# Stick-breaking attention whose mask and tail are summed in PSUM, with two sets of banks, three heads in flight, and a convolution that begins one stage earlier

## The reference, cut to what matters

```python
def stick_breaking_attention(q, k, v):          # 512 tokens, 8 heads of 64
    z = jnp.einsum("bqhd,bkhd->bhqk", qb, kb) * scale
    mask = s_idx < t_idx
    log_beta = jax.nn.log_sigmoid(z)
    log_one_minus = jnp.where(mask, jax.nn.log_sigmoid(-z), 0.0)
    tail = lax.cumsum(log_one_minus, axis=3, reverse=True) - log_one_minus
    weights = jnp.where(mask, jnp.exp(log_beta + tail), 0.0)
    outs.append(jnp.einsum("bhqk,bkhd->bqhd", weights, vb))
...
attn = stick_breaking_attention(q, k, v).reshape(bsz, seq, ATTN_WIDTH)
c = glu_a * jax.nn.sigmoid(glu_b)
c = causal_depthwise_conv(c, conv_dw_w[layer], conv_dw_b[layer])     # 31 taps, 512 channels
c = jax.nn.silu(layer_norm(c, conv_ln_g[layer], conv_ln_b[layer]))
mixed = jnp.concatenate([attn, c], axis=-1) @ w_out[layer]
```

## Time and profile before

| | |
|---|---|
| three runs | 3109.27, 3105.01, 3108.11 us; median 3108.11 |
| the profiled execution | 3104.05 us, span 3102.3 us, granted clock 0.96 |
| busy share of the span | PE 93%, PEld 76%, DVE 48%, ACT 32%, POOL 45% |
| 156 us to 327 us from the start: busy | PE 103.93, DVE 139.95, ACT 72.72, POOL 89.74 of 171.00 us, granted clock 0.78 |

### The profile page before, as it was taken

How to read it: one execution, slowest core, us unless ns; L and a number is a source line. 1 busy time by engine, 2 the same in 40 slices (tenths; PEclk the granted TensorE clock), 3 DMA queues, 4 the chain that set the end, 5 groups by cost and what they waited for, 6 DMA issues and landing times.

```text
span 3102.3 us, 35547 instructions
## 1 busy us (share of the span) xinstructions
PE 2888.4 (93%) x13578; PEld 2348.8 (76%) x13578; DVE 1501.8 (48%) x2421; ACT 995.7 (32%) x1447; POOL 1393.4 (45%) x550
## 2 busy tenths in 40 slices
PE   7956799998998989988998999999999999999997
PEld 5733587886795668776887888888888888888886
DVE  3189432122117541546978788650002555555554
ACT  3234332223115542333333333332223223222322
POOL 5492254454320014443346777774445444444441
PEclk9968899999996999989999999999999999999999
DMA  3200122322420002321243654655455666556662
GB/s 124 92 3 0 41 82 88 102 89 74 151 82 14 1 28 95 108 82 55 75 143 103 207 158 156 207 176 185 147 196 170 195 191 195 193 189 190 195 195 70
DMA packets 222319, 375.90 MB, mean 121 GB/s; under 512 B 11152, under 2 KB 142608, under 8 KB 211216
## 3 DMA queue, kind: packets, MB, share of 16 engines
q1 hardware_dynamic: 222224, 374.68, 36.8%
HBM read 305.43 MB, written 69.21 MB: 121 GB/s over the span
## 4 chain that ended last, share of the span: by engine, by line
PE 77%; DVE 8%; issue 7%; POOL 5%; ACT 2%; DMA 0%; POOLq 0%; SPq 0%; DVEq 0%; ACTq 0%
PE bank L254 15%; PE bank L255 15%; PE bank L256 15%; PE bank L1831 8%; PE bank L1832 8%; PE bank L1833 8%; POOL rows_b L1647 4%; DVE cacc L433 2%; PE bank L1163 2%; PE bank L1134 2%; PE bank L1811 1%; PE bank L1143 1%; POOL u_lo L1611 1%; DVE xl L397 1%; PE bank L1753 0%
## 5 line engine op out<-in xcount | busy, mean ns | idle before, releaser
L246 POOL TENSOR_TENSOR w_lo<-w_raw,w_hi 128x2048 fp32r<-128x2048 f32 (+2 forms) x96 | 418.4, 4360 | 804.3 <-ACT w_hi L241 804.2
L1998 DVE TENSOR_TENSOR h_lo<-h_raw,h_hi 128x512 fp32r<-128x512 f32 x128 | 308.9, 2413 | 351.3 <-ACT h_hi L1633 351.3
L1628 POOL TENSOR_TENSOR v_lo<-v_raw,v_hi 128x1024 fp32r<-128x1024 f32 x128 | 308.0, 2407 | 377.4 <-ACT v_hi L1624 377.4
L1611 POOL TENSOR_TENSOR u_lo<-u_raw,u_hi 128x1024 fp32r<-128x1024 f32 x128 | 325.0, 2539 | 338.9 <-ACT u_hi L1605 338.9
L254 PE MATMUL bank<-xh,w_lo 128*128 128x512 f32 x1056 | 421.6, 399 | 38.5 <-DVE xl L397 18.1
L255 PE MATMUL bank<-xl,w_hi 128*128 128x512 f32 x1056 | 417.3, 395 | 0.0
L256 PE MATMUL bank<-xh,w_hi 128*128 128x512 f32 x1056 | 416.6, 395 | 0.0
L254 PE MATMUL bank<-xh,u_lo 128*128 128x512 f32 x1024 | 404.4, 395 | 0.3 <-POOL u_lo L1611 0.3
L1831 PE MATMUL bank<-h_hi,v_lo 128*128 128x512 f32 x1024 | 399.6, 390 | 4.2 <-DVE h_lo L1998 4.2
L1832 PE MATMUL bank<-h_lo,v_hi 128*128 128x512 f32 x1024 | 399.3, 390 | 0.0
L1833 PE MATMUL bank<-h_hi,v_hi 128*128 128x512 f32 x1024 | 399.3, 390 | 0.0
(11 more groups left out here) (338 smaller groups left out, 4492.4 us busy)
## 6 DMA issues: line engine op xcount, KB each, us to landing
w_raw<-w_small SPq DMA_DIRECT2D x80, 1024.0 KB, 4.9
u_raw<-expert_u SPq DMA_DIRECT2D x128, 512.0 KB, 3.7
v_raw<-expert_v SPq DMA_DIRECT2D x128, 512.0 KB, 5.1
h_scratch<-h_act SPq DMA_DIRECT2D x128, 256.0 KB, 2.2
g_scratch<-stage SPq DMA_DIRECT2D x8, 4096.0 KB, 16.7
h_raw<-h_scratch SPq DMA_DIRECT2D x128, 256.0 KB, 2.7
g_in<-g_scratch SPq DMA_DIRECT2D x64, 512.0 KB, 4.1
w_raw<-w_small SPq DMA_DIRECT2D x8, 768.0 KB, 4.3
```

The costliest lines, as they stand in the source:

```text
L246: pool.tensor_tensor(wl[g % 2][:, :n], raw[g % 2][:, :n], wh[g % 2][:, :n].bitcast(F32), ALU.subtract).then_inc(sem("lo_done"), 1)
L1611: pool.tensor_tensor(u_lo[c % 2][:, :, :], u_raw[c % 4][:, :, :], u_hi[c % 2][:, :, :].bitcast(F32), ALU.subtract)\
L1628: pool.tensor_tensor(v_lo[c % 4][:, :], v_raw[c % 4][:, :], v_hi[c % 4][:, :].bitcast(F32), ALU.subtract)\
L1998: dve.tensor_tensor(h_lo[c % 4][:, :], h_raw[c % 4][:, :], h_hi[c % 4][:, :].bitcast(F32), ALU.subtract)\
```

## The change

It does five things.

1. Scores, mask and tail of a head are summed in the same PSUM banks. After the four score matmuls, four bf16 matmuls of an identity with a constant add -2^100 where a key is not before its query. `tails` adds minus the softplus over the key itself and all later ones (`from_key`, `all_keys`) to the same banks. ACT takes the Exp straight from PSUM. With that `lbeta`, `log_weights` and both masks on DVE go.
2. Even heads use banks 4 to 6, odd heads banks 0 to 2; `scores(h+2)` waits until the weights of head h have been read.
3. The order of the heads: PE runs `tails(h)`, `values(h-1)`, `scores(h+2)`; ACT the weights of h, the output of h-1, `pre(h+2)`; DVE 12 instructions of the convolution and `softplus(h+2)`.
4. DVE begins the convolution in the `in_v` stage, three instructions after each of the eight copies, 24 in all. POOL begins its group before it prepares the two first blocks of `out1`, not after. The inverses are spread in the order of the pairs of heads, and only after all eight tiles of `in_v` have been copied.
5. The rounding of the attention's output for `out1` goes with each second head, and three of the four low parts are taken before the layer norm's reciprocal. PE takes the mean after the values of head 5. Three constants more are written at the start.

```diff
+        def head_banks(h):
+            return (lin_bank if h % 2 else att_bank)[:3]
+
+        PAIR_ORDER = (0, 4, 1, 5, 2, 6, 3, 7)
...
                 if h >= 1:
-                    act.wait_ge(sem("st_zread"), h)
+                    act.wait_ge(sem("st_soft"), h)
                 for b, (off, w) in enumerate(PIECES):
-                    ins = act.activation(ln1[:, off:off + w], att_bank[b][:, :w], ACT.Abs)
...
+            def weights_out(h):
+
+                act.wait_ge(sem("st_tail"), h + 1)
+                if h >= 2:
+                    act.wait_ge(sem("st_pv"), h - 1)
+                for b, (off, w) in enumerate(PIECES):
+                    ins = act.activation(wgt[h % 2][:, off:off + w], head_banks(h)[b][:, :w], ACT.Exp)
+                ins.then_inc(sem("st_w"), 1)
...
+                if h % 2:
+                    act.wait_ge(sem("st_o"), h + 1)
+                    act.activation(xh[:, k, :], attn[:, k, :], ACT.Copy).then_inc(sem("mix1_hi"), 1)
...
             pre(0)
-            for h in range(HEADS + 1):
-                if h + 1 < HEADS:
-                    pre(h + 1)
...
+            pre(1)
+            for h in range(HEADS):
+                weights_out(h)
                 if h >= 1:
-                    r = (h - 1) % 2 * HD
-                    act.wait_ge(sem("st_pv"), h)
-                    act.activation(attn[r:r + HD, (h - 1) // 2, :], lin_bank[3][r:r + HD, :], ACT.Copy)\
-                       .then_inc(sem("st_o"), 1)
+                    head_out(h - 1)
+                if h + 2 < HEADS:
+                    pre(h + 2)
...
+            head_out(HEADS - 1)
...
-            act.wait_ge(sem("st_o"), HEADS)
-            for k in range(CT):
-                act.activation(xh[:, k, :], attn[:, k, :], ACT.Copy).then_inc(sem("mix1_hi"), 1)
...
-            for b in range(1, LAYER["out1"]["block"] + 2):
...
             wait(pool, ("bank_free", 4 + 16), ("params_loaded", 16))
             conv_pool(pool)
-            for b in range(LAYER["out1"]["block"] + 2, LAYER["up0"]["block"] + 2):
+            for b in range(LAYER["out1"]["block"], LAYER["up0"]["block"] + 2):
...
-            for j in range(8):
-                if j >= 2:
-                    pe.wait_ge(sem("qk_ready"), j - 1)
-                pe.matmul(att_bank[1 + j % 2][:, :], head_spread[:, j * P:(j + 1) * P], rstd16[:, :],
...
+            pe.wait_ge(sem("bank_free"), 4 + LAYER["in_v"]["tile"] + 8)
+
+            def spread(first, last):
+                for n in range(first, last):
+                    j = PAIR_ORDER[n]
+                    if n >= 2:
+                        pe.wait_ge(sem("qk_ready"), n - 1)
+                    pe.matmul((att_bank, lin_bank)[n % 2][3][:, :], head_spread[:, j * P:(j + 1) * P], rstd16[:, :],
+                              start=True, stop=True).then_inc(sem("qk_spread"), 1)
...
-                pe.wait_ge(sem("qk_ready"), 8)
-                if h >= 1:
-                    pe.wait_ge(sem("st_zread"), h)
+                pe.wait_ge(sem("qk_ready"), 2 * t + 2)
...
                 for kb in range(QT):
                     b, c, w = regions(kb)
-                    last = pe.matmul(att_bank[b][:, c:c + w], qk[r:r + HD, 4 + t, kb * P:(kb + 1) * P],
-                                     qk[r:r + HD, t, kb * P:S], start=True, stop=True)
+                    bank = head_banks(h)[b]
+                    pe.matmul(bank[:, c:c + w], qk[r:r + HD, 4 + t, kb * P:(kb + 1) * P], qk[r:r + HD, t, kb * P:S],
+                              start=(c == 0), stop=False, skip_group_check=True)
+                for kb in range(QT):
+                    b, c, w = regions(kb)
+                    last = pe.matmul(head_banks(h)[b][:, c:c + P], ident_b[:, :], not_before[:, :], start=False, stop=True,
+                                     skip_group_check=True)
                 last.then_inc(sem("st_z"), 1)
...
                 pe.wait_ge(sem("st_soft"), h + 1)
-                if h >= 1:
-                    pe.wait_ge(sem("st_logw"), h)
-                else:
-                    pe.wait_ge(sem("bank_free"), 4 + LAYER["in_v"]["tile"] + 8)
                 for kb in range(QT):
                     b, c, w = regions(kb)
...
                         wj = S - jb * P
-                        last = pe.matmul(lin_bank[b][:, c + w - wj:c + w], later_key[:, :] if jb == kb else ones[:, :],
-                                         soft[h % 2][:, KOFF[jb]:KOFF[jb] + wj], start=(jb == kb), stop=(jb == QT - 1))
+                        last = pe.matmul(head_banks(h)[b][:, c + w - wj:c + w], from_key[:, :] if jb == kb else all_keys[:, :],
+                                         soft[h % 2][:, KOFF[jb]:KOFF[jb] + wj], start=False, stop=True, skip_group_check=True)
                 last.then_inc(sem("st_tail"), 1)
...
                 r = h % 2 * HD
-                pe.wait_ge(sem("st_wm"), h + 1)
+                pe.wait_ge(sem("st_w"), h + 1)
...
+            spread(0, 4)
             scores(0)
-            for h in range(HEADS + 1):
-                if h + 1 < HEADS:
-                    scores(h + 1)
-                if h < HEADS:
-                    tails(h)
-                if h == HEADS:
-                    variance()
+            spread(4, 8)
+            pe.wait_ge(sem("qk_ready"), 8)
+            scores(1)
+            for h in range(HEADS):
+                tails(h)
                 if h >= 1:
                     values(h - 1)
-                if h == HEADS - 1:
+                if h + 2 < HEADS:
+                    scores(h + 2)
+                if h == HEADS - 2:
                     mean()
+            values(HEADS - 1)
+            variance()
...
+            dve.wait_ge(sem("bank_free"), 4 + 16)
...
-            for j in range(8):
-                dve.wait_ge(sem("qk_spread"), j + 1)
+                conv_dve(dve, 3 * n, 3 * n + 3)
+            for n, j in enumerate(PAIR_ORDER):
+                dve.wait_ge(sem("qk_spread"), n + 1)
                 gain = qg[:, 0:1] if j < 4 else col("k_norm")
-                dve.scalar_tensor_tensor(out=qk[:, j, :], in0=qk[:, j, :], scalar=gain, in1=att_bank[1 + j % 2][:, :],
+                dve.scalar_tensor_tensor(out=qk[:, j, :], in0=qk[:, j, :], scalar=gain, in1=(att_bank, lin_bank)[n % 2][3][:, :],
                                          op0=ALU.mult, op1=ALU.mult).then_inc(sem("qk_ready"), 1)
...
                 for b, (off, w) in enumerate(PIECES):
-                    ins = dve.scalar_tensor_tensor(out=soft[h % 2][:, off:off + w], in0=att_bank[b][:, :w], scalar=0.0,
+                    ins = dve.scalar_tensor_tensor(out=soft[h % 2][:, off:off + w], in0=head_banks(h)[b][:, :w], scalar=0.0,
                                                    in1=ln1[:, off:off + w], op0=ALU.max, op1=ALU.add)
-                for b, (off, w) in enumerate(PIECES):
-                    ins = dve.scalar_tensor_tensor(out=lbeta[h % 2][:, off:off + w], in0=att_bank[b][:, :w], scalar=0.0,
-                                                   in1=ln1[:, off:off + w], op0=ALU.min, op1=ALU.subtract)
-                ins.then_inc(sem("st_zread"), 1)
-                dve.wait_ge(sem("st_zread"), h + 1)
-                mask_diagonals(soft[h % 2]).then_inc(sem("st_soft"), 1)
...
-                for b, (off, w) in enumerate(PIECES):
-                    ins = dve.tensor_tensor(wgt[h % 2][:, off:off + w], lbeta[h % 2][:, off:off + w],
-                                            lin_bank[b][:, :w], ALU.subtract)
-                ins.then_inc(sem("st_logw"), 1)
+                ins.then_inc(sem("st_soft"), 1)
 
             softplus(0)
-            per_head = -(-N_CONV // (HEADS - 1))
-            for h in range(HEADS + 1):
-                conv_dve(dve, h * per_head, (h + 1) * per_head)
-                if h >= 1:
-                    dve.wait_ge(sem("st_w"), h)
...
+            softplus(1)
+            per_head = -(-(N_CONV - 24) // (HEADS - 2))
+            for h in range(HEADS - 2):
+                conv_dve(dve, 24 + h * per_head, 24 + (h + 1) * per_head)
+                softplus(h + 2)
...
+            for k in range(CT - 1):
+                mixed_low(k)
             dve.wait_ge(sem("ln_std"), 1)
             chain.link(dve.reciprocal(ln_rstd[:, :], ln_std[:, :]))
             for k in range(CT):
                 dve.tensor_tensor(cacc[:, k, :], cacc[:, k, :], ln_rstd[:, :], ALU.mult).then_inc(sem("ln_y"), 1)
-                mixed_low(k)
+                if k == 0:
+                    mixed_low(CT - 1)
...
+            step(pool.memset(all_keys[:, :], -1.0))
+            step(pool.affine_select(out=from_key[:, :], in_=all_keys[:, :], compare_op=ALU.is_ge, fill=0.0, base=0,
                                     pattern=[[-1, P]], channel_multiplier=1))
-            step(pool.affine_select(out=causal[:, :], in_=ones[:, :], compare_op=ALU.is_gt, fill=0.0, base=0,
+            step(pool.memset(not_before[:, :], 0.0))
```

(2 more changed lines are left out.)

48 lines of the change are left out of this document (18 added, 30 removed).

## The result

| | before | changed |
|---|---|---|
| median of the runs on one chip | 3106.56 us | 3059.61 us (3058.56 to 3063.07, four runs) |
| ratio | | 0.9854, 95% interval 0.9841 to 0.9866 |
| the profiled execution, span | 3104.05, 3102.3 us | 3063.07, 3061.3 us |
| layer norm's reciprocal starts | 326.53 us | 279.86 us |
| first residual addition of `out1` | 339.72 us | 292.05 us |

The account below looks back on a forecast made before the run. The prediction took DVE's full queue to bound the attention stage. 49.2 us gained up to the reciprocal, plus 1.0 in out1, less 0.9 for constants, made 49.3 us from 3108.11: forecast 3058 us, range 3046 to 3078.

Parts of the forecast that it names:

- The cause: Attention heads' stage: DVE's full queue bounds it, so the 40.7 us of work removed there shorten the time.
- The start: From in_v to softplus(1): scores of head 0 about 5 us later, DVE idle twice, 20 us in sum, softplus(1) done at 187.2.
- the constants: Three more constants written on POOL at the kernel's start, on the path: 0.6 to 1.5 us, taken as 0.9.
- The heads: Softplus(2) to softplus(7): DVE needs 14.75 us a head beside POOL, 9.6 after; ACT's 10.7 gradually takes over; softplus(7) ends at 259.6.
- POOL's two weight blocks (4.50 each ...) now come after its convolution ... cost nothing: POOL's preparation of out1 weights: moved behind its convolution, still some 60 us before out1 wants them, priced at zero.
- The end: From softplus(7) to the layer norm's reciprocal, at 277.3 us instead of 326.53, plus 1 us gained in out1's first tile.
- the four mask matmuls of a head: bf16 matmuls on PE behind each head's scores: between 0 and about 0.95 us a head, taken as 0.3.
- The ledger: DVE from its first v tile to the last softplus: some 180 us before, 134.7 after.
- (a): PE's clock stays at 1.2 GHz throughout the attention stage, making the kernel slower: 3111.5 or 3115.5 us; chance 0.04.
- (b): PE's clock is low in half of the attention stage's bursts, costing some 13 us: 3072 us; chance 0.17.
- (c): Early convolution in in_v delays the spreads by as much as it saves later: 3064 us; chance 0.10.
- (d): PE's clock does not fall at the spreads, so softplus(1) comes 8.6 us earlier: 3050 us; chance 0.14.

Follow-up runs that it names:

- the second profile of the change: The changed kernel, unaltered, run and profiled once more on the same chip as later follow-ups: median 3060.08 us, ratio 0.9856 to the kernel before.

## Why the prediction was right, step by step

**The cause.** "What leaves that queue leaves the time until something else is late" held: log beta's 12.9 us of DVE work, put back, cost 8 us in the profile and 11.9 by the medians, and what the profile doesn't charge fell into stretches in which DVE idled. But the sentence says too little about what the second bank set does: with one set something else is late at once, and the same removal brings 11 in all. The sum had both in it and so came out right.

**The start** was 3 us cheaper than forecast. The 24 early instructions took 22.7 us, not 26.4, as the three right behind the reciprocal went at 0.66 and three more at 0.73; the eighth copy came at 150.64 (forecast 154), the first product at 154.19 (157.5), scores(0) at 158.68 (161.4), and softplus(1) ended at 185.2 (187.2, or 188.1 with the constants; the times before it carry the constants' 0.8 too). The two idle stretches of DVE are there as foretold, 6.36 and 10.29 and some smaller waits, 22 in sum (20), and filling them was worth 8.

**The heads** lost it again, and this is the step that failed. "POOL's two weight blocks (4.50 each ...) now come after its convolution ... cost nothing" looked only at who waits for the blocks and not at what stands beside them. I had given DVE 1.10 us beside POOL whatever POOL does; beside the two 128x2048 subtractions one convolution instruction took 4.98 and one 3.47. The blocks cost 7.0 us of DVE, on its path. Even the 1.10 is a mean: beside POOL's convolution single instructions take 0.74, 1.17 or 1.75. POOL also ended its convolution at 226.8 and not 221, since it began 0.8 later and since beside DVE's first pieces one of its instructions took 5.71 and the next 2.39 (elsewhere the two kinds take 1.56 to 1.88 and 1.26 to 1.80). So softplus(4) ended at 233.8 (231.3), softplus(5) at 246.0 (240.8), softplus(7) at 263.8 (259.6).

```profile
133.10 5.71 POOL L454 TENSOR_SCALAR conv_prod<-cpad,params_sb 128x512 f32<-128x512 f32 x1
```

**The end** went as worked out: from the last softplus's end to the reciprocal 16.0 us, forecast 17.7; the first tile of `out1` 12.19 behind the reciprocal where it was 13.19. That this is just the 1.0 that was forecast is luck: it was picked out of 0 to 5, and in the second profile of the change it is 1.6. Reciprocal 279.86 and 283.38, forecast 278.2. The constants cost 0.8 (ACT's first rounding starts at 14.13; forecast 0.9), the four mask matmuls of a head 0.61 and 0.40 at the two clocks (0.3), ACT's Exp out of PSUM 1.36 (1.4).

```profile
163.24 0.61 PE L628 MATMUL bank<-not_before,ident_b 128*128 128x128 bf16 x4
...
202.65 0.40 PE L628 MATMUL bank<-not_before,ident_b 128*128 128x128 bf16 x4
```

**The ledger**: from DVE's first v copy to the end of its last softplus 138.0 us against 134.7 forecast: 2.9 less at the start, 6.2 more in the heads (7.2 in the pieces beside the blocks, 1.0 less in the last). The end took 1.7 less. Errors of opposite sign nearly cancelled, so that the stage came out 1.7 us long in this profile; that the total is so near is in part luck, and without the experiments it would have hidden them. The total was also worked out from a median of 3108.11 for the kernel before, which with a fourth run is 3106.56: the gain was forecast as 49.3 us and is 46.95.

**The rivals.** (a) PE at 1.2 GHz throughout: no, the mean granted clock from 180 us to the reciprocal is 0.88 (0.85 in the second profile), far above the 0.56 at which the case would decide, and 1.00 from 240 to 280. PE waited 7.10 us ahead of `tails(4)`, and the clock from 230 to 235 is 0.50, 1.00 again later. By "TensorE: Matmul & The Clock Gate" of the Trainium skill, section on HAM oscillation, gaps between bursts bring it down; these rows agree. Short gaps do not foretell it: behind the same 1.21 us of waiting ahead of the scores of head 7 the clock fell in one profile of the change and not in the other. (b) came true for one burst that counts in one of two profiles, 3.5 us; the bursts at the low clock earlier (0.53 from 215 to 220) stand beside full pieces of DVE, where the prediction says that nothing is lost. (c) is refuted by the kernel without early convolution. (d) didn't occur: 0.50 from 150 to 175; its price was not isolated.

## What to carry to other kernels

A block of work moved on an engine that "has time" must also be priced by what runs beside it on the engine that has none: look for the same engine's instruction at each kind of neighbour, not for one mean pace. When work leaves a full queue, ask which ring of waits (here scores, tails, weights on one set of banks) takes over: with one set of banks the rest of the change gained 11 us, with two 47. After the change, list the bottleneck engine's idle stretches and fill them with its own backlog: that and moving POOL's blocks gave another 14 us.
